# Second mixer: the strips alternate between two pairs of accumulator banks, and the state's projections and one more output turn go to the three rotating banks

## The chip, the cores and the metric

The kernel runs on one core of a Trainium2 chip, as one launch. Its time is the device time of that launch in microseconds. The core has a matrix engine (TensorE, PE in the rows), a vector engine (VectorE, DVE), an activation engine (ScalarE, ACT), a general engine (GpSimd, POOL), and a queue that issues the transfers (SyncE, SP). TensorE writes only to PSUM, which has eight banks of 128 partitions x 512 float32 values; VectorE and ScalarE read the banks. The engines run each its own program in its own order, and wait for one another on semaphores.

## The reference, cut to what matters

The whole computes two blocks on 256 tokens of width 1024: a first block of two layers (feed-forward, a mixer, cross attention, feed-forward) and a second block. The change lies in the mixer of the second block:

```python
h = rms_norm_2(x, norm_mix[l])
qa, ka, va, u, qm, km, vm, gates = split_in(h @ w_in[l])
oa = swa_attention(qa, ka, va, sinks, slopes_swa)      # window of 128, 8 heads, a sink per head
ya = oa @ w_o_swa[l]
ys = s5_ssm(u, lam_re, lam_im, log_step, b_re, b_im, c_re, c_im, d_skip)   # 32 groups x 64 complex states
z = jax.nn.gelu(ys) @ w_glu[l]
yb = (z[..., :512] * jax.nn.sigmoid(z[..., 512:])) @ w_o_ssm[l]
om = moba_attention(qm, km, vm, slopes_moba)           # one block of 256 keys, 8 heads
yc = om @ w_o_moba[l]
g = jax.nn.sigmoid(gates)                              # three gates of width 1024
x = x + (g[..., :1024] * ya + g[..., 1024:2048] * yb + g[..., 2048:] * yc) @ w_out[l]
```

The reshapes to heads are left out. After it come a feed-forward layer with a squared ReLU and the last norm.

## The kernel before, in words

**Products.** Every weight is used in two halves, a high one (`whi`) and a low one (`wlo`), and a product of activations and weights is three matmuls (high by high, low by high, high by low: lines 445 to 447). Weights come in pieces of 128 x 1024 values: SyncE loads a piece into one of five buffers `raw`, ScalarE copies its high half (line 1118), VectorE subtracts to get the low half (line 1677), and TensorE multiplies. There are three buffers for the halves. Each engine's program makes the halves of piece j + 2 while TensorE is to work on piece j.

**Strips.** A strip is 512 columns of an output for all 256 tokens. A strip of kind `both` has two row blocks t = 0, 1 of 128 tokens, each of which accumulates in one bank over all of the strip's pieces, so it holds a pair of banks. `gemm_piece` (line 449) runs one piece; at a strip's first piece it takes the pair that it is told, or `next_pair()`.

**Who holds a bank.** `open_bank(b)` makes TensorE wait for the events in `free[b]`, the signals by which the last user's reader said that it is done, and `free[b]` is set when a user has issued its last matmul. `turn_bank()` hands out three rotating banks in turn. In the second mixer these are banks 3, 4 and 5; bank 7 holds the weighed values; before the change bank 6 is the state projections' own, and the strips go round the pairs (1, 2), (0, 1), (2, 0).

**The second mixer** (`second`, line 963 for TensorE, 1530 for ScalarE, 2472 for VectorE). After the strip `su` comes a loop over `MIXED`, 40 weight pieces s = 0 to 39 in a fixed order: sk (0, 1), sqa (2 to 5), sv (6, 7), sqm (8 to 11), the strips of the gates gate0 (12 to 15), gate1 (16 to 19), gate4 (20 to 23), gate5 (24 to 27), gate2 (28 to 31), gate3 (32 to 35), and swa0 (36, 37), swa1 (38, 39). Each of the four engines walks over the same s, and does beside the piece what the tables say:
- `DRIVEN_AT`: at every even s from 2 to 32 a drive k (0 to 15), the input matmuls of a state group (line 1030). VectorE reads its bank twice (lines 2533, 2534, event `back`), GpSimd combines, VectorE scans (2544), rotates (2547, 2548), GpSimd combines.
- `SCORED_AT`: at every even s from 8 to 30 the scores of an attention item (line 582). VectorE reads the bank (line 1856, event `biased`) and takes the maxima; ScalarE exponentiates (line 1207). At s + 1 TensorE transposes the probabilities (`prob_turn`, line 564), ScalarE copies them out at its s + 2 (line 1226, event `copied_a`), and at s + 3 TensorE weighs the values (line 611).
- Four drives later, after pieces 12, 20, 28 and 36, `project(J)` (line 1035, matmuls of line 1042) projects four state groups, and VectorE reads the result one step later (line 2552, event `scan`).
- `OUT_AT`: after pieces 24, 25, 35 and 36 TensorE transposes half an attention output (`out_turn`, line 544). ScalarE takes the high half out (line 1163), VectorE the low one (line 1768, event `alo`).
- After a gate strip's last piece ScalarE copies its two banks out, with the row scale or straight with the sigmoid (line 1552, event `gate`). Gelu and sigmoid need another activation table than the exponential.

Within an even s TensorE opens the drive's bank, then the score's, and only then issues the two kinds of matmuls by turns; the piece, `project`, the weighing, the transposes and the output turn follow in this order. After the loop come the strips glu1, glu0, moba0, ssm0, moba1, ssm1 and the output projection so0, so1, on the pairs (0, 1) and (2, 3), with rotating banks 4, 5 and 6.

Of the kernel before, what the change touches and what calls it, by code (L numbers as in the profile page):

```python
# [412 lines left out]
def pe_program(K, G, A):  # L413

    S, T = K.S, K.nc.tensor
    pe = Engine(T)
    ident, banks = K.ident, K.banks
    free = [()] * 8
    turn_n, pair_n, pairs = [0], [0], [((0, 2), (1, 3))]

    def open_bank(b):
        for event in free[b]:
            pe.wait_ge(*event)
        free[b] = ()

    def turn_bank():
        turn_n[0] += 1
        b = (3 if len(pairs[0]) == 3 else 4) + turn_n[0] % 3
        open_bank(b)
        return b  # L430

# [48 lines left out]
    def gemm(name, after0, after1, pair=None, beside={}):  # L480

        g = G[name]
        for n in range(g.n):
            gemm_piece(g, n, pair)
            if n in beside:
                beside[n]()
        free[K.place[name][0]], free[K.place[name][1]] = (after0,), (after1,)
# [473 lines left out]
        project_x("o", "oo", "x1")  # L961

    def second():
        pairs[0], pair_n[0] = ((1, 2), (0, 1), (2, 0)), 1
        gemm("su", S.copied_d.at(("su", 0)), S.copied_d.at(("su", 1)), None, {0: lambda: norm_turns("s", "f3", True, (2, 3))})
        b = turn_bank()
        K.place["spread"] = b
        for t in range(2):
# [37 lines left out]
        def mixed_piece(name, n):  # L1006
            if name in ("sk", "sv"):
                (keys_piece if name == "sk" else values_piece)(n)
                return
            gemm_piece(G[name], n, (2, 0) if name[:2] == "sq" else None)  # L1010
            if n == G[name].n - 1:
                for t in range(2):
                    free[K.place[name][t]] = ((S.gate.at((int(name[4]), t)) if name[:4] == "gate" else
                                               S.gated.at((0, int(name[3]), t)) if name[:3] == "swa" else S.copied_a.at((name, t))),)
# [18 lines left out]
                free[b] = (S.back.at(k),)  # L1033

        def project(J):
            open_bank(6)
            pe.wait_ge(*S.proj.at(0))
            pe.wait_ge(*S.turned_forth.at(4 * J + 3))
            for ri in range(2):
                for k in range(4 * J, 4 * J + 4):  # L1040
                    cs = slice(32 * BLOCKS[k % 4], 32 * BLOCKS[k % 4] + 32)
                    ins = T.matmul(banks[6][cs, 0:256], K.CL[ri][:, J, cs], K.state[k % 7][:, ri, :], start=ri == 0, stop=ri == 1,
                                   skip_group_check=True)
            ins.then_inc(*S.projected.done(J))
            free[6] = (S.scan.at(("z", J)),)
        for s, (name, n) in enumerate(MIXED):
            k = DRIVEN_AT.get(s)
            if k is not None and k != 1:
# [21 lines left out]
                prob_turn("mA" if i >= 6 else "sA", i % 6, 4)  # L1070
            if s in OUT_AT:
                a, _, g = OUT_AT[s]
                spare = [b for b in range(3) if b not in K.place[name]] if s == 25 else [None]
                out_turn(a, 0, K.O, lambda t, g: S.weighed.at((a, t)), (g,), spare[0])

        def gated(branch):
            return [[S.gated.at((branch, c, t)) for t in range(2)] for c in range(2)]
        pairs[0] = ((0, 1), (2, 3))
        gemm("glu1", S.silu.at(("glu", 0)), S.silu.at(("glu", 1)))
        gemm("glu0", S.product.at(("glu", 0)), S.product.at(("glu", 1)))  # L1080
        gemm("moba0", *gated(2)[0])
# [581 lines left out]
def dve_program(K, G, A):  # L1663
# [3 lines left out]
    banks = K.banks  # L1667
# [804 lines left out]
    def second():  # L2472
# [76 lines left out]

        def state_out(J):  # L2550
            dve.wait_ge(*S.projected.at(J))
            V.scalar_tensor_tensor(out=zin[:, J, :], in0=K.uT[:, J, :], scalar=K.gain(108 + J), in1=banks[6][:, 0:256],
                                   op0=ALU.mult, op1=ALU.add).then_inc(*S.scan.done(("z", J)))
        r8 = K.stat("r8", 2)
        for s, (name, n) in enumerate(MIXED):
# [402 lines left out]
```

## Time and profile before

| | us |
|---|---|
| median of three timed runs | 1626.81 |
| lowest, highest | 1624.32, 1627.30 |
| the profiled execution's own time | 1623.05 |
| its span | 1621.8 |
| TensorE busy | 1595.5 (98%) |
| VectorE busy | 1109.3 (68%) |
| ScalarE busy | 861.6 (53%) |
| GpSimd busy | 227.5 (14%) |

The span is that of one profiled execution, from its first to its last instruction; the time around it is 1.25 us more. Matmuls are pipelined: a matmul's own duration is longer than the distance to the next one's start, so the distances between starts tell how fast TensorE goes, and a short hole can stand there without showing as idle. A row's bracket gives the idle time of the engine before it and what ended it. In the timeline a row merges several like instructions (x2, x4).

### The profile page before, as it was taken

The page shows a single profiled execution, that of the slowest core. Times are in us where ns is not written, and L with a number is a line of the kernel's source. Part 1 is how long each engine was busy: PE and PEld are TensorE (multiplying, and loading weights), DVE is VectorE, ACT ScalarE, POOL GpSimd, SP SyncE. Part 2 cuts the span into 40 slices and gives each one's busy share as a digit, 9 for nine tenths or more (in the row PEclk, how much of TensorE's full clock was granted, in tenths as well). Part 3 has the DMA queues.
Part 4 walks back from the last instruction along what each step waited for, and adds up shares of the span by engine and source line. Part 5 has one row for each costly group of instructions (what it writes and reads, how often), then busy time and mean ns, then how long its engine had stood idle before and what let it go on. Part 6 is the DMA issues. An engine that isn't in the chain of part 4 may idle for free.

```text
span 1621.8 us, 21203 instructions
## 1 busy us (share of the span) xinstructions
PE 1595.5 (98%) x8050; PEld 1331.2 (82%) x8050; DVE 1109.3 (68%) x1769; ACT 861.6 (53%) x1324; POOL 227.5 (14%) x351
## 2 busy tenths in 40 slices
PE   8999999999999999999999999999999999999998
PEld 6888877788888888888889888888889877888886
DVE  6775788867655556555596775655568997776566
ACT  5554556855545445444555555544454457454444
POOL 2499901000000000000000000000014442100000
PEclk9999999999999999999999999999999999999999
DMA  9766656445455565655654553555685554556563
GB/s 283 242 208 213 207 169 191 150 142 156 140 185 188 188 186 178 191 185 190 213 171 156 163 186 111 183 187 187 189 261 166 165 157 143 182 194 193 188 188 109
DMA packets 187543, 295.22 MB, mean 182 GB/s; under 512 B 13510, under 2 KB 108144, under 8 KB 186160
## 3 DMA queue, kind: packets, MB, share of 16 engines
q1 hardware_dynamic: 183264, 275.93, 54.4%
q0 software_dynamic: 3888, 17.60, 3.4%
q8 instruction: 64, 1.05, 0.3%
q10 hardware_dynamic: 288, 0.33, 0.1%
q14 instruction: 39, 0.32, 0.1%
HBM read 288.29 MB, written 5.25 MB: 181 GB/s over the span
## 4 chain that ended last, share of the span: by engine, by line
PE 86%; DVE 8%; ACT 3%; issue 2%; POOL 1%; DMA 0%; SPq 0%; DVEq 0%; ACTq 0%
PE b L445 25%; PE b L447 24%; PE b L446 24%; PE b L667 4%; DVE wlo L1677 2%; PE b L669 2%; ACT whi L1118 1%; PE b L690 1%; PE b L920 1%; PE b L902 1%; PE b L511 1%; PE b L527 1%; PE b L611 1%; PE b L564 1%; ACT R L1207 1%
## 5 line engine op out<-in xcount | busy, mean ns | idle before, releaser
L1677 DVE TENSOR_TENSOR wlo<-raw,whi 128x1024 fp32r<-128x1024 f32 (+1 forms) x523 | 648.7, 1243 | 430.6 <-ACT whi L1118 429.2
L1118 ACT ACTIVATE whi<-raw 128x1024 fp32r<-128x1024 f32 (+1 forms) x523 | 549.8, 1053 | 554.3 <-PE b L447 518.4
L445 PE MATMUL b<-whi,hT 128*128 128x512 f32 (+1 forms) x1040 | 413.0, 397 | 9.4 <-DVE wlo L1677 8.2
L447 PE MATMUL b<-whi,hT 128*128 128x512 f32 (+1 forms) x1040 | 404.8, 389 | 0.0
L446 PE MATMUL b<-wlo,hT 128*128 128x512 f32 (+1 forms) x1040 | 404.3, 389 | 0.0
L445 PE MATMUL b<-whi,oT 128*128 128x512 f32 x672 | 265.1, 394 | 0.0
L447 PE MATMUL b<-whi,oT 128*128 128x512 f32 x672 | 262.0, 390 | 0.0
L446 PE MATMUL b<-wlo,oT 128*128 128x512 f32 x672 | 261.6, 389 | 0.0
L445 PEld LDWEIGHTS b<-whi,hT 128*128 128x128 f32 x1040 | 195.8, 188 | 54.7 <-DVE wlo L1677 10.4
L447 PEld LDWEIGHTS b<-whi,hT 128*128 128x128 f32 x1040 | 195.7, 188 | 41.6
L446 PEld LDWEIGHTS b<-wlo,hT 128*128 128x128 f32 x1040 | 196.0, 188 | 37.7
L447 PEld LDWEIGHTS b<-whi,oT 128*128 128x128 f32 x672 | 126.1, 188 | 26.9
L445 PEld LDWEIGHTS b<-whi,oT 128*128 128x128 f32 x672 | 126.2, 188 | 26.2 <-DVE R L2501 0.5
L446 PEld LDWEIGHTS b<-wlo,oT 128*128 128x128 f32 x672 | 126.3, 188 | 25.3
L667 PE MATMUL b<-hT,whi 128*128 128x512 f32 x256 | 90.8, 399 | 0.0
L1207 ACT ACTIVATE R<-R,st 128x256 f32<-128x256 f32 (+1 forms) x96 | 43.5, 455 | 73.3 <-DVE st L1861 30.5
L669 PE MATMUL b<-hT,wlo 128*128 128x256 f32 x256 | 71.9, 281 | 0.0
L2822 POOL DMA_DIRECT2D biasB<-in_rel x1 | 0.5, 527 | 490.8 <-PE b L690 490.8
L1249 ACT ACTIVATE biasA<-b,st 128x256 f32<-128x256 f32 x88 | 41.1, 474 | 44.6 <-PE b L447 41.2
L445 PE MATMUL b<-hT,whi 128*128 128x256 f32 (+1 forms) x216 | 62.2, 288 | 0.1
L446 PE MATMUL b<-hT,whi 128*128 128x256 f32 (+1 forms) x216 | 61.1, 283 | 0.0
L447 PE MATMUL b<-hT,wlo 128*128 128x256 f32 (+1 forms) x216 | 61.0, 283 | 0.0
(349 smaller groups left out, 1855.9 us busy)
## 6 DMA issues: line engine op xcount, KB each, us to landing
raw<-in_ffn_w_in SPq DMA_DIRECT2D x350, 256.0 KB, 3.2
raw<-in_ffn_w_out SPq DMA_DIRECT2D x88, 512.0 KB, 3.4
raw<-in_w_ff SPq DMA_DIRECT2D x64, 512.0 KB, 4.0
raw<-in_w_in SPq DMA_DIRECT2D x36, 512.0 KB, 3.7
raw<-in_x_w_kv SPq DMA_DIRECT2D x32, 512.0 KB, 4.1
raw<-in_even_w_in SPq DMA_DIRECT2D x24, 512.0 KB, 4.2
raw<-in_odd_w_in SPq DMA_DIRECT2D x24, 512.0 KB, 4.0
raw<-in_x_w_q SPq DMA_DIRECT2D x16, 512.0 KB, 4.1
```

Source lines behind the costliest of these rows:

```text
L445: T.matmul(out, ah, bh, start=start, stop=False, skip_group_check=skip)
L446: T.matmul(out, ah, bl, start=False, stop=False, skip_group_check=skip)
L447: return T.matmul(out, al, bh, start=False, stop=stop, skip_group_check=skip)
L511: ins = T.transpose(banks[b][:, (2 * i + t) * P:(2 * i + t + 1) * P], src[:, t, kt * P:(kt + 1) * P], ident)
L527: ins = T.transpose(banks[b][:, i * P:(i + 1) * P], K.sqj[t][:, i * P:(i + 1) * P], ident)
L564: ins = T.transpose(banks[b][:, k * P:(k + 1) * P], src[:, k * P:(k + 1) * P], ident)
L667: T.matmul(bank[:, :].rearrange("p (a t) -> p a t", a=2), hi[:, kk, cs], K.hs[:, :, kt, :], start=kt == 0, stop=False, skip_group_check=True)
L669: ins = T.matmul(bank[:, 256:512], lo[:, kk, cs], K.hT[0][:, kt, :], start=False, stop=kt == 7, skip_group_check=True)
L1118: E.activation(K.whi[j % NSPLIT][:, 0:n], K.raw[j % NRAW][:, 0:n], ACT.Copy).then_inc(*S.whi.done(j))
L1207: ins = E.activation(s3[:, h, :], s3[:, h, :], ACT.Exp, bias=nm[:, h:h + 1], accum_out=sm[h])
L1249: E.activation(s[:, 0:256], bank[:, 0:256], ACT.Silu, scale=K.stat(("y", f.name), 2)[:, t:t + 1]).then_inc(*S.silu.done((f.name, c, t)))
L1677: V.tensor_tensor(K.wlo[j % NSPLIT][:, 0:n], K.raw[j % NRAW][:, 0:n], K.whi[j % NSPLIT][:, 0:n].bitcast(F32), ALU.subtract).then_inc(*S.wl ...
```

## The change

The pairs of the second mixer's strips become (0, 1) and (2, 6), used by turns. `su` is told the pair (2, 0), which it had before, sqa is told (6, 0) instead of (2, 0), and sqm (2, 6). The keys and values stay in bank 1. `project(J)` takes `turn_bank()` instead of bank 6, and VectorE's `state_out` reads it from there. The output turn after piece 25, which took the one of banks 0 to 2 that no strip held, takes `turn_bank()` too. The first rotating bank is kept in `turn_first` and not worked out from the number of pairs. Since `su` no longer takes a pair from the rotation and there are two pairs and not three, the strips after the loop start on the other of their two pairs. No engine's instructions change or move; what changes is the bank in them and the waits ahead of them.

```diff
--- before.py
+++ after.py
@@ -416,7 +416,7 @@
     pe = Engine(T)
     ident, banks = K.ident, K.banks
     free = [()] * 8
-    turn_n, pair_n, pairs = [0], [0], [((0, 2), (1, 3))]
+    turn_n, turn_first, pair_n, pairs = [0], [4], [0], [((0, 2), (1, 3))]
 
     def open_bank(b):
         for event in free[b]:
@@ -425,7 +425,7 @@
 
     def turn_bank():
         turn_n[0] += 1
-        b = (3 if len(pairs[0]) == 3 else 4) + turn_n[0] % 3
+        b = turn_first[0] + turn_n[0] % 3
         open_bank(b)
         return b
 
@@ -961,8 +961,8 @@
         project_x("o", "oo", "x1")
 
     def second():
-        pairs[0], pair_n[0] = ((1, 2), (0, 1), (2, 0)), 1
-        gemm("su", S.copied_d.at(("su", 0)), S.copied_d.at(("su", 1)), None, {0: lambda: norm_turns("s", "f3", True, (2, 3))})
+        pairs[0], pair_n[0], turn_first[0] = ((0, 1), (2, 6)), 1, 3
+        gemm("su", S.copied_d.at(("su", 0)), S.copied_d.at(("su", 1)), (2, 0), {0: lambda: norm_turns("s", "f3", True, (2, 3))})
         b = turn_bank()
         K.place["spread"] = b
         for t in range(2):
@@ -1007,7 +1007,7 @@
             if name in ("sk", "sv"):
                 (keys_piece if name == "sk" else values_piece)(n)
                 return
-            gemm_piece(G[name], n, (2, 0) if name[:2] == "sq" else None)
+            gemm_piece(G[name], n, {"sqa": (6, 0), "sqm": (2, 6)}.get(name))
             if n == G[name].n - 1:
                 for t in range(2):
                     free[K.place[name][t]] = ((S.gate.at((int(name[4]), t)) if name[:4] == "gate" else
@@ -1033,16 +1033,16 @@
                 free[b] = (S.back.at(k),)
 
         def project(J):
-            open_bank(6)
+            b = K.place["project", J] = turn_bank()
             pe.wait_ge(*S.proj.at(0))
             pe.wait_ge(*S.turned_forth.at(4 * J + 3))
             for ri in range(2):
                 for k in range(4 * J, 4 * J + 4):
                     cs = slice(32 * BLOCKS[k % 4], 32 * BLOCKS[k % 4] + 32)
-                    ins = T.matmul(banks[6][cs, 0:256], K.CL[ri][:, J, cs], K.state[k % 7][:, ri, :], start=ri == 0, stop=ri == 1,
+                    ins = T.matmul(banks[b][cs, 0:256], K.CL[ri][:, J, cs], K.state[k % 7][:, ri, :], start=ri == 0, stop=ri == 1,
                                    skip_group_check=True)
             ins.then_inc(*S.projected.done(J))
-            free[6] = (S.scan.at(("z", J)),)
+            free[b] = (S.scan.at(("z", J)),)
         for s, (name, n) in enumerate(MIXED):
             k = DRIVEN_AT.get(s)
             if k is not None and k != 1:
@@ -1070,12 +1070,11 @@
                 prob_turn("mA" if i >= 6 else "sA", i % 6, 4)
             if s in OUT_AT:
                 a, _, g = OUT_AT[s]
-                spare = [b for b in range(3) if b not in K.place[name]] if s == 25 else [None]
-                out_turn(a, 0, K.O, lambda t, g: S.weighed.at((a, t)), (g,), spare[0])
+                out_turn(a, 0, K.O, lambda t, g: S.weighed.at((a, t)), (g,))
 
         def gated(branch):
             return [[S.gated.at((branch, c, t)) for t in range(2)] for c in range(2)]
-        pairs[0] = ((0, 1), (2, 3))
+        pairs[0], turn_first[0] = ((0, 1), (2, 3)), 4
         gemm("glu1", S.silu.at(("glu", 0)), S.silu.at(("glu", 1)))
         gemm("glu0", S.product.at(("glu", 0)), S.product.at(("glu", 1)))
         gemm("moba0", *gated(2)[0])
@@ -2549,7 +2548,7 @@
 
         def state_out(J):
             dve.wait_ge(*S.projected.at(J))
-            V.scalar_tensor_tensor(out=zin[:, J, :], in0=K.uT[:, J, :], scalar=K.gain(108 + J), in1=banks[6][:, 0:256],
+            V.scalar_tensor_tensor(out=zin[:, J, :], in0=K.uT[:, J, :], scalar=K.gain(108 + J), in1=banks[K.place["project", J]][:, 0:256],
                                    op0=ALU.mult, op1=ALU.add).then_inc(*S.scan.done(("z", J)))
         r8 = K.stat("r8", 2)
         for s, (name, n) in enumerate(MIXED):
```

TensorE's order at the transposes of piece 25 and the drive and score of piece 26, before (L611 weighs, L564 transposes the probabilities, L544 is the output turn, L1030 the drive, L582 the score; b0 to b7 are the banks):

```order
L611 MATMUL b7<-R1 128x64 x4
L564 MATMUL b5<-cst,R1 128x128 [waits s_exped,s_back]
L564 MATMUL b5<-cst,R1 128x128 x3
L544 MATMUL b0<-cst,O 128x128 [waits s_gate]
L544 MATMUL b0<-cst,O 128x128 x3
L1030 MATMUL b3<-vsb,BT 128x256 [waits s_alo,s_biased]
L582 MATMUL b4<-R1 128x256
L1030 MATMUL b3<-vsb,BT 128x256
L582 MATMUL b4<-R1 128x256
```

and after:

```order
L611 MATMUL b7<-R1 128x64 x4
L564 MATMUL b4<-cst,R1 128x128 [waits s_exped,s_back]
L564 MATMUL b4<-cst,R1 128x128 x3
L544 MATMUL b5<-cst,O 128x128 [waits s_biased]
L544 MATMUL b5<-cst,O 128x128 x3
L1030 MATMUL b3<-vsb,BT 128x256 [waits s_copied_a,s_alo]
L582 MATMUL b4<-R1 128x256
L1030 MATMUL b3<-vsb,BT 128x256
L582 MATMUL b4<-R1 128x256
```

The output turn (L544) has moved from bank 0 to bank 5. The probabilities are in bank 4 instead of 5, and that is the bank that the score of piece 26 takes next, so the drive's wait has gained `s_copied_a`.

TensorE's order between the projection after piece 12 and the drive and score of piece 14 (the twelve matmuls of piece 13 and L1042, the projection, stand before this), before:

```order
L611 MATMUL b7<-R1 128x64 [waits s_copied_a]
L611 MATMUL b7<-R1 128x64 x3
L564 MATMUL b4<-cst,R1 128x128 [waits s_exped]
L564 MATMUL b4<-cst,R1 128x128 x3
L1030 MATMUL b5<-vsb,BT 128x256 [waits s_biased,s_back]
L582 MATMUL b3<-R1 128x256
L1030 MATMUL b5<-vsb,BT 128x256
L582 MATMUL b3<-R1 128x256
```

and after, where L1042 is in bank 4 instead of 6:

```order
L611 MATMUL b7<-R1 128x64 x4
L564 MATMUL b5<-cst,R1 128x128 [waits s_exped,s_back]
L564 MATMUL b5<-cst,R1 128x128 x3
L1030 MATMUL b3<-vsb,BT 128x256 [waits s_scan,s_biased]
L582 MATMUL b4<-R1 128x256
L1030 MATMUL b3<-vsb,BT 128x256
L582 MATMUL b4<-R1 128x256
```

The drive went from bank 5 to 3 and the score from bank 3 to 4, the projection's bank, and the wait has gained `s_scan`. The same stands at pieces 22 and 30.

TensorE's order at the first piece of gate3 (piece 32), before:

```order
L1030 MATMUL b3<-vsb,BT 128x256 [waits s_back]
L1030 MATMUL b3<-vsb,BT 128x256
L445 MATMUL b2<-whi2,hT 128x512 [waits s_gate,s_wlo]
L446 MATMUL b2<-wlo2,hT 128x512
L447 MATMUL b2<-whi2,hT 128x512
L445 MATMUL b0<-whi2,hT 128x512 [waits s_gate]
L446 MATMUL b0<-wlo2,hT 128x512
```

and after:

```order
L1030 MATMUL b4<-vsb,BT 128x256 [waits s_back]
L1030 MATMUL b4<-vsb,BT 128x256
L445 MATMUL b2<-whi2,hT 128x512 [waits s_gate,s_wlo]
L446 MATMUL b2<-wlo2,hT 128x512
L447 MATMUL b2<-whi2,hT 128x512
L445 MATMUL b6<-whi2,hT 128x512 [waits s_gate]
L446 MATMUL b6<-wlo2,hT 128x512
```

The second row block went from bank 0, which gate2 had just filled, to bank 6, which gate5 had. Both waits are for `s_gate`, but for different values of it.

## Rows read from the trace of the kernel before

**Rows 1.** The page's part 1: busy us, share of the span, instructions

```profile
PE 1595.5 (98%) x8050; PEld 1331.2 (82%) x8050; DVE 1109.3 (68%) x1769; ACT 861.6 (53%) x1324; POOL 227.5 (14%) x351
```

**Rows 2.** Busy time by stretch: length, each engine's busy us, TensorE's clock, DMA

```profile
1205.00:1377.00 172.00, 168.42 (x1092) 142.12 (x1091) 154.65 (x243) 96.71 (x186) 64.98 (x80) 1.00 0.55 165
```

**Rows 3.** Waits of TensorE, 1205 to 1440: total us, times, longest

```profile
PE b L445 <- ACT biasB L1552: 1.2, 1, 1.2
```

**Rows 4.** Timeline, pieces 25 and 26: start, duration, engine, line [idle before <-releaser]

```profile
1323.29 0.60 PE L544 MATMUL b<-cst,O 128*128 128x128 f32 x4
1323.59 0.68 DVE L1768 TENSOR_TENSOR oT<-b,oT 128x512 fp32r<-128x512 f32 x1
1323.93 0.60 ACT L1163 ACTIVATE oT<-b 128x512 fp32r<-128x512 f32 x1 [1.42 <-PE b L544]
...
1324.42 0.45 PE L1030 MATMUL b<-vsb,BT 64*128 64x256 f32 x1 [0.53 <-DVE oT L1768]
1324.42 1.05 ACT L1118 ACTIVATE whi<-raw 128x1024 fp32r<-128x1024 f32 x1
...
1325.37 0.58 ACT L1226 ACTIVATE R<-b 128x512 f32<-128x512 f32 x1
```

**Rows 5.** Timeline, drive of piece 14 and the first projection's read

```profile
1273.27 0.48 PE L1030 MATMUL b<-vsb,BT 64*128 64x256 f32 x1
...
1273.30 0.48 DVE L2552 SCALAR_TENSOR_TENSOR vsb<-vsb,gcol,b 128x256 f32<-128x256 f32 x1
...
1274.02 0.38 PE L1030 MATMUL b<-vsb,BT 64*128 64x256 f32 x1
...
1274.84 0.69 DVE L2533 TENSOR_TENSOR R<-b,M 128x512 f32<-128x512 f32 x1
```

**Rows 6.** Timeline, drive of piece 22 and the second projection's read

```profile
1306.51 0.48 DVE L2552 SCALAR_TENSOR_TENSOR vsb<-vsb,gcol,b 128x256 f32<-128x256 f32 x1
...
1306.72 0.48 PE L1030 MATMUL b<-vsb,BT 64*128 64x256 f32 x1
```

**Rows 7.** Timeline, drive of piece 30 and the third projection's read

```profile
1340.41 0.48 DVE L2552 SCALAR_TENSOR_TENSOR vsb<-vsb,gcol,b 128x256 f32<-128x256 f32 x1
...
1341.77 0.48 PE L1030 MATMUL b<-vsb,BT 64*128 64x256 f32 x1
```

**Rows 8.** Timeline, first products of gate3 (piece 32) and gate2's copies

```profile
1351.43 0.40 PE L447 MATMUL b<-whi,hT 128*128 128x512 f32 x1
...
1352.31 1.27 ACT L1552 ACTIVATE biasB<-b,st 128x512 f32<-128x512 f32 x2
...
1353.05 0.50 PE L445 MATMUL b<-whi,hT 128*128 128x512 f32 x1 [1.23 <-ACT biasB L1552]
...
1353.39 0.39 PE L446 MATMUL b<-wlo,hT 128*128 128x512 f32 x1
...
1353.62 0.40 PE L447 MATMUL b<-whi,hT 128*128 128x512 f32 x1
```

**Rows 9.** Timeline, low half of piece 35 and TensorE's first product of it

```profile
1359.52 1.22 DVE L1677 TENSOR_TENSOR wlo<-raw,whi 128x1024 fp32r<-128x1024 f32 x1
...
1361.62 0.39 PE L445 MATMUL b<-whi,hT 128*128 128x512 f32 x1
```

**Rows 10.** Timeline, first products of swa1 (piece 38)

```profile
1372.36 0.39 PE L447 MATMUL b<-whi,oT 128*128 128x512 f32 x1
...
1372.80 0.50 PE L445 MATMUL b<-whi,oT 128*128 128x512 f32 x1
```

**Rows 11.** Timeline, two products near the start, and a wait of TensorE at 208 us

```profile
7.15 0.63 PE L445 MATMUL b<-whi,hT 128*128 128x512 f32 x1
7.58 0.63 PE L446 MATMUL b<-wlo,hT 128*128 128x512 f32 x1
...
208.29 1.38 PE L511 MATMUL b<-cst,O 128*128 128x128 f32 x8 [2.22 <-DVE O L1747]
```

**Rows 12.** Busy time of the stretch 205 to 210 us, columns as in rows 2

```profile
205.00:210.00 5.00, 2.72 (x16) 1.94 (x15) 4.48 (x17) 2.52 (x3) 0.87 (x2) 1.00 0.52 213
```

## The prediction

> **What bounds the kernel now.** I read the page first. TensorE is busy 98% of the span [rows 1], so a change in the second mixer can move the end only through time in which TensorE stands still there. The busy time by stretches shows the mixer: between 1205 and 1377 us TensorE is busy for 168.42 of 172.00 us, VectorE for 154.65, at a granted clock of 1.00 [rows 2]. So TensorE leads, VectorE follows with 90%, and at most 3.6 us are there to be won, of which the waits name the owners: 1.2 us for a gate copy of ScalarE (a strip's bank) [rows 3], 0.5 us for a low half of VectorE (a rotating bank) [rows 4]; one more wait, for a softmax exponential, hangs on data and not on a bank, and the change leaves it alone. Then I laid the waits which the change writes against the timeline: for every bank, when its old user lets go of it, and when TensorE comes to it.
>
> The weight pieces of the mixer have the numbers 0 to 39 here, in their order in MIXED. TensorE issues twelve 128x512 products for a piece, 0.23 us apart (1353.39, 1353.62) [rows 8].
>
> **Strips on two pairs (removes waits).** Before, neighbouring strips share one of the banks 0, 1, 2, so a strip's second row block must wait for the copy out of the strip before. That costs time at one place, the start of gate3 (piece 32): the product at 1351.43 would be followed by one at 1351.66, but it comes at 1353.05, when the first of the two gate activations that start at 1352.31 is over [rows 8]. 1353.05 - 1351.66 = 1.39 us. After, gate3 has banks 2 and 6, whose last user was gate5, a whole strip earlier. ScalarE does not get faster by it, though: the weight chain for the pieces behind was set by ScalarE and GpSimd. The low half of piece 35's weights is written by VectorE from 1359.52 to 1360.74, and TensorE takes piece 35 at 1361.62 [rows 9]. If TensorE is 1.39 us ahead it comes at 1360.23 and must wait until about 1360.74 + 0.15 = 1360.89: 0.66 us are given back. (0.15 us is what lay between the end of VectorE's low half, 1323.59 + 0.68 = 1324.27, and TensorE's start at 1324.42 [rows 4].) What stands before that low half on VectorE works on the state and waits for GpSimd and ScalarE there, not for TensorE, so it does not move up with it. Net gain 0.73 us; bounds 0 (all given back) and 1.39 (nothing).
> A smaller one of the same kind is at swa1 (piece 38): 1372.80 after 1372.36 instead of 1372.59 [rows 10], 0.21 us, because bank 1 was still swa0's. After, swa1 has gate3's banks, which ScalarE has emptied during swa0. Gain 0.21 us; bounds 0 and 0.21. The other strip starts show no idle time before, and lose only waits that were met.
>
> **The state's projections in a rotating bank (adds waits).** Project had bank 6 for itself. Now it takes the next of 3, 4, 5, and a rotating bank comes round after three takers. Project(J) is issued after pieces 12, 20 and 28, and the third taker after it is the score of pieces 14, 22 and 30. In program order that score's wait stands before the drive matmul (both banks are opened first), so TensorE stands still with the drive too until VectorE has read the projection (L2552).
> First: VectorE ends it at 1273.30 + 0.48 = 1273.78, TensorE starts the drive at 1273.27 [rows 5]. New start 1273.78 + 0.15 = 1273.93, cost 0.66 us.
> Second: 1306.51 + 0.48 = 1306.99 against 1306.72 [rows 6], alone 0.42 us with the 0.15. But TensorE is then already 0.66 us late and VectorE less so: its next read of a drive bank (1274.84) has to wait for the drive that ended at 1274.02 + 0.38 = 1274.40, now 0.66 later, plus an estimated 0.1 us for the release, 1275.16, so VectorE slips by 0.32 [rows 5]. 0.42 + 0.32 - 0.66 = 0.08 us.
> Third: 1340.41 + 0.48 = 1340.89 against 1341.77 [rows 7]: met, 0.9 us to spare.
> Together 0.74 us; bounds 0 (if the release comes well before the end that the profile shows) and 1.08 (0.66 + 0.42, if VectorE slips as far as TensorE). The two other new waits of this part are met by far: project itself wants a copy of ScalarE that is long done, and the transposes of the probabilities want VectorE's read of a drive bank, which stands a whole piece earlier in its order.
>
> **The output turn of piece 25 in a rotating bank (adds the largest wait).** Before, it took a free strip bank (bank 0 in the order's rows). Now it is one more taker between the probabilities' transposes of the same piece and the drive and score of piece 26. So the score of piece 26 gets the bank whose probabilities TensorE has only just transposed, and ScalarE must have copied them out. ScalarE is busy in that order: it takes the high half of the output turn (1323.93, it waited for TensorE's transposes from 1323.29), then the high half of a weight piece (1324.42), and copies the probabilities from 1325.37 to 1325.95 [rows 4]. TensorE starts piece 26's drive at 1324.42, having already waited 0.5 us for the low half of the other output turn. ScalarE's release reaches TensorE fast (two gate activations from 1352.31 take 0.7 us for the first, and TensorE goes on at 1353.05 [rows 8]), so 0.04 us are added: 1325.95 + 0.04 - 1324.42 = 1.57 us. ScalarE's three instructions all hang on TensorE's own transposes, so the wait moves along with whatever TensorE lost before; nothing else in the way hides it. Bounds: 0.62 (if the weight piece between, 1324.42 to 1325.37, fell out of the chain) and 1.98 (with as much again as a piece's first product comes late by after such a wait, 1353.39 - 1353.05 - 0.23 = 0.11 us [rows 8], and the 0.3 us by which VectorE slipped at piece 14). While TensorE stands, VectorE runs dry too: its read of the drive's result waits for the later drive. VectorE is then closer behind TensorE, which is why the third projection stays met; it does not cost on its own, since the weights' low halves are made two pieces ahead.
>
> **Sum.** 0.74 + 1.57 - 0.73 - 0.21 = +1.37 us. On the profiled execution's own 1623.05 us (span 1621.8) that gives 1624.4. The three timed runs have a median of 1626.81, 3.8 us above that execution, and I add the difference to it: 1626.81 + 1.37 = 1628.2 us, +0.08%. From no change this kernel's measurement can tell about 0.2%, 3.3 us (the three runs alone differ by 3 us), so the forecast is: no change that shows, on the slow side of it.
>
> The Trainium skill, "Perfetto Trace Analysis", section "Matmuls", says that independent matmul groups should rotate through different PSUM banks, so that the emptying of one overlaps the next one's products. By that rule the change would gain the whole 1.39 us of gate3 and cost nothing. The trace agrees with it for the strips, but the same rule speaks against the other half of the change, which puts five more groups on the same three banks.
>
> **Rivals.**
> A, the gain stays whole and the new waits are short. For it: only one bank wait of the mixer has a price above 1 us now [rows 3], and ScalarE has idle time in the mixer, so it may come to the copy earlier. Against it: three instructions of ScalarE in a row, of which the first waits for TensorE [rows 4]. It gives -1.39 - 0.21 + 0.62 = -0.98 us, 1625.8 us.
> B, VectorE becomes the bound. With 154.65 of 172.00 us busy [rows 2] it has little room, and each of TensorE's new waits starves it (0.3 us at piece 14, more at piece 26). If as much as the wait at piece 26 costs, 1.57 us, comes back once more as waits of TensorE for low halves of weights, and piece 35 eats up all of gate3's gain, the sum is 0.74 + 1.57 - 0.21 + 1.57 = +3.7 us: 1630.5, slower. It decides from the point where a low half ends less than 0.1 us before TensorE wants it; at 1360.74 against 1361.62 [rows 9] there are 0.88 us, elsewhere more, and that speaks against it.
> C, the clock falls. At piece 26 TensorE would be idle from 1323.29 + 0.60 = 1323.89 to 1325.99, 2.1 us. At the lower level the products come every 0.43 us (7.15, 7.58) instead of 0.23 [rows 11]; if the 24 products of pieces 26 and 27 ran so, that is 24 x 0.20 = 4.8 us more, +6.2 in all, 1633.0 us. Against it: before 208.29 TensorE waited 2.22 us and the granted clock of that stretch is 1.00 [rows 11, 12]. The Trainium skill, "TensorE: Matmul & The Clock Gate", section "HAM oscillation — how this bites in real kernels", says that idle gaps between bursts of matmuls can throttle the clock; this trace shows none that did so by its length.
>
> **How the numbers follow.** Forecast 0.74, A 0.14, B 0.08, C 0.04. The likeliest time is 1628.2. The terms' bounds give 0 + 0.62 - 1.39 - 0.21 = -0.98 to 1.08 + 1.98 - 0 - 0 = +3.1, and a median of a few runs moves by 1 us or so by itself: 1625.2 to 1631.0, which takes in A and B and leaves out C. Faster by over 0.2% would need 3.3 us, more than all bank waits of the mixer hold: 0.03, for the scatter alone. Slower by over 0.2%: C, half of B, and some scatter on top of a forecast that is already at +1.4: 0.13. Within: 0.84.
>
> **What would show it.** In the profile after: TensorE's drive of piece 26 waits for ScalarE's copy of the probabilities (L1226) for about 2 us where it waited 0.5 us for VectorE; the drives of pieces 14 and 22 wait for VectorE's projection read, about 0.6 and 0 us; the wait for the gate activation at gate3 is gone and a wait for the low half of weights of about 0.6 us has come two or three pieces later; the granted clock stays at 1.00. If no wait for L1226 shows at piece 26, the largest term is wrong; if low halves are waited for at more than one place, it is B.

## The result, and the profile after

| us | before | after |
|---|---|---|
| median (executions) | 1624.79 (12) | 1626.83 (12) |
| lowest, highest | 1622.57, 1627.30 | 1625.63, 1629.15 |
| the profiled execution's own time | 1623.05 | 1626.74 |
| its span | 1621.8 | 1625.4 |
| its mean granted clock | 0.999 | 0.997 |

The ratio is 1.0016, with a 95% interval of [1.0009, 1.0024]: 0.0016 x 1625 = 2.6 us slower, a loss clear of the scatter but within the 0.2% that the forecast called no change. A second comparison, with the same kernel on another occasion, gave 1.0020 [1.0012, 1.0029] (e0_again below). The forecast was +1.37 us and 1628.2 us. The time itself came out 1.4 us below the forecast although the loss came out larger, and that the two are so close is luck: the three runs on which the forecast stood (median 1626.81) were long ones for this kernel, whose medians in the comparisons are 1624.79, 1623.59 and 1623.40. The base was 1626.81 - 1624.79 = 2.0 us too high, while the loss by medians, 2.04 us, was 0.7 us more than forecast. One of the 33 executions of the kernel before that stand beside e3, e4, e5 and e7 took 1987.04 us at a granted clock of 0.753, and the ratios leave it out.

Lines of VectorE and ScalarE have a number lower by one in the kernel after: L1225 copies the probabilities, L2551 reads the projection, L1676 writes the low halves. The page's part 1, after, against [rows 1]:

```profile
PE 1598.0 (98%) x8050; PEld 1334.1 (82%) x8050; DVE 1109.2 (68%) x1769; ACT 861.7 (53%) x1324; POOL 227.5 (14%) x351
```

The instructions are the same, and yet TensorE is busy 2.5 us longer: waits alone would have made it stand still, not work longer. Some matmuls must have run slower. The busy time by stretches, with the granted clock as the third number from the end, shows where; the row of 1205 to 1377 us answers to [rows 2], and before has 1.00 in every one of these stretches:

```profile
206.00:212.00 6.00, 3.73 (x13) 3.01 (x13) 5.57 (x15) 4.43 (x7) 0.26 (x1) 0.73 0.67 226
328.00:334.00 6.00, 5.17 (x29) 4.28 (x29) 5.85 (x11) 3.10 (x7) 0.00 (x0) 1.00 0.31 90
...
1205.00:1377.00 172.00, 166.64 (x1081) 140.70 (x1079) 152.21 (x240) 94.66 (x185) 64.93 (x80) 0.99 0.56 164
...
1328.00:1330.00 2.00, 2.00 (x11) 1.20 (x8) 0.96 (x2) 0.00 (x0) 0.05 (x1) 0.58 0.95 314
1330.00:1332.00 2.00, 2.00 (x7) 1.57 (x6) 1.93 (x5) 0.00 (x0) 1.43 (x2) 0.56 0.21 81
1332.00:1334.00 2.00, 2.00 (x11) 1.64 (x10) 2.00 (x3) 1.42 (x5) 0.00 (x0) 1.00 0.00 0
```

The clock has fallen at two places, near 208 us and at piece 26. TensorE's waits inside the mixer, after, against [rows 3]:

```profile
PE b L1030 <- ACT R L1225: 2.2, 1, 2.2
PE b L564 <- ACT st L1215: 1.6, 1, 1.6
PE b L1030 <- DVE vsb L2551: 0.8, 2, 0.6
PE b L445 <- DVE wlo L1676: 0.5, 1, 0.5
```

The gate's wait (1.2 us, biasB) is gone. The wait for the softmax exponential (L1215) is the one that hangs on data, and has stayed at 1.6. The other three rows are the new ones of the prediction. Their places in the timeline, against [rows 5], [rows 6], [rows 7], [rows 4], [rows 8], [rows 9] and [rows 10] in that order (rows between those shown are left out, here and below):

```profile
1273.93 0.47 DVE L2551 SCALAR_TENSOR_TENSOR vsb<-vsb,gcol,b 128x256 f32<-128x256 f32 x1
1274.55 0.45 PE L1030 MATMUL b<-vsb,BT 64*128 64x256 f32 x1 [0.57 <-DVE vsb L2551]
...
1307.69 0.47 DVE L2551 SCALAR_TENSOR_TENSOR vsb<-vsb,gcol,b 128x256 f32<-128x256 f32 x1
1308.31 0.45 PE L1030 MATMUL b<-vsb,BT 64*128 64x256 f32 x1 [0.27 <-DVE vsb L2551]
...
1344.66 0.48 DVE L2551 SCALAR_TENSOR_TENSOR vsb<-vsb,gcol,b 128x256 f32<-128x256 f32 x1
1346.48 0.48 PE L1030 MATMUL b<-vsb,BT 64*128 64x256 f32 x1
...
1324.80 0.60 PE L544 MATMUL b<-cst,O 128*128 128x128 f32 x4
1324.97 0.68 DVE L1767 TENSOR_TENSOR oT<-b,oT 128x512 fp32r<-128x512 f32 x1
1325.44 0.60 ACT L1162 ACTIVATE oT<-b 128x512 fp32r<-128x512 f32 x1 [1.56 <-PE b L544]
1325.93 1.05 ACT L1117 ACTIVATE whi<-raw 128x1024 fp32r<-128x1024 f32 x1
1326.88 0.59 ACT L1225 ACTIVATE R<-b 128x512 f32<-128x512 f32 x1
1327.61 0.45 PE L1030 MATMUL b<-vsb,BT 64*128 64x256 f32 x1 [2.21 <-ACT R L1225]
1328.95 0.79 PE L445 MATMUL b<-whi,hT 128*128 128x512 f32 x1
1329.54 0.63 PE L446 MATMUL b<-wlo,hT 128*128 128x512 f32 x1
...
1356.14 0.40 PE L447 MATMUL b<-whi,hT 128*128 128x512 f32 x1
1356.38 0.40 PE L445 MATMUL b<-whi,hT 128*128 128x512 f32 x1
...
1364.22 1.22 DVE L1676 TENSOR_TENSOR wlo<-raw,whi 128x1024 fp32r<-128x1024 f32 x1
1365.49 0.50 PE L445 MATMUL b<-whi,hT 128*128 128x512 f32 x1 [0.50 <-DVE wlo L1676]
...
1376.39 0.39 PE L447 MATMUL b<-whi,oT 128*128 128x512 f32 x1
1376.61 0.39 PE L445 MATMUL b<-whi,oT 128*128 128x512 f32 x1
```

The first product of gate3's second row block comes 0.24 us after the one before it (1356.14, 1356.38), where there were 1.62 us, and at swa1 the product that came 0.44 us after its neighbour comes 0.22 us after it (1376.39, 1376.61): both strips find their banks empty. Such a comparison is read by distances: one takes the start of the same matmul in both traces, and where the difference changes, time was lost or won. That gives this account of 3.69 us between the two profiled executions (1626.74 - 1623.05):

| place | start before, after | difference | changes by | predicted |
|---|---|---|---|---|
| on entering the mixer (clock, 208 us) | | 0.64 | +0.64 | not the change's |
| drive of piece 14 | 1273.27, 1274.55 | 1.28 | +0.64 | +0.66 |
| drive of piece 22, and what it gave back | 1306.72, 1308.31 | 1.59, then 1.51 | +0.23 | +0.08 |
| output turn, drive of piece 26 | 1324.42, 1327.61 | 3.19 | +1.68 | +1.57 |
| drive of piece 30 (clock, piece 26) | 1341.77, 1346.48 | 4.71 | +1.52 | 0 |
| gate3, with piece 34 as the place it is read | | 3.21 | -1.50 | -1.39 |
| past piece 35's first product | | 4.02 | +0.81 | +0.66 |
| past swa1, to the end | | 3.68 | -0.34 | -0.21 |

Without the two rows of the clock it is 0.64 + 0.23 + 1.68 - 1.50 + 0.81 - 0.34 = +1.52 us, where +1.37 was forecast.

### The profile page after: what moved, and what is told of

The parts are those of the page before. It is cut to its first block and busy times, and to the rows that moved or that the text cites. A ratio compares the mean times of both kernels' runs of the same rounds, so it can differ in the third digit from the quotient of the medians.

```text
span 1625.4 us, 21204 instructions
## 1 busy us (share of the span) xinstructions
PE 1598.0 (98%) x8050; PEld 1334.1 (82%) x8050; DVE 1109.2 (68%) x1769; ACT 861.7 (53%) x1324; POOL 227.5 (14%) x351
## 5 line engine op out<-in xcount | busy, mean ns | idle before, releaser
L1676 DVE TENSOR_TENSOR wlo<-raw,whi 128x1024 fp32r<-128x1024 f32 (+1 forms) x523 | 648.6, 1243 | 430.7 <-ACT whi L1117 429.6
```

The lines of the kernel that those rows point to most:

```text
L1676: V.tensor_tensor(K.wlo[j % NSPLIT][:, 0:n], K.raw[j % NRAW][:, 0:n], K.whi[j % NSPLIT][:, 0:n].bitcast(F32), ALU.subtract).then_inc(*S.wl ...
```

## The experiments

Theory: the time after is the sum of the three kinds of waits as forecast, and on top of it the granted clock falls behind the long wait at piece 26 and costs some 1.5 us. Rival: the wait alone costs what is seen, and the lower clock is another of the falls that this kernel has anyhow, at one place or another, whatever the change does. Each kernel was timed in five rounds against the kernel before. Since falls of the clock come and go between executions, I look in each profile at the clock at three places: 206 to 212 us, 328 to 334 us, and about piece 26.

**e0_again**: the changed kernel once more, unedited.

> The changed kernel once more, beside the others, for its time on this chip and for a second profile. Theory (wait and clock): it takes 2 to 3.5 us more than before; TensorE waits 2.2 us for the copy of line 1225 at piece 26, and the granted clock falls to about 0.57 for 3 to 4 us behind it, so that some six products come 0.43 us apart. Rival (the fall was an accident of one execution): the wait is there, the clock stays at 1.00, and the time is 1.5 us less than in the profile, +1.4 us over before.

Median 1627.5 (11 executions, lowest 1625.63), before 1623.59 (31, lowest 1622.72), ratio 1.0020 [1.0012, 1.0029]. The clock is 1.00 at the first two places, and falls again at piece 26:

```profile
206.00:212.00 6.00, 3.71 (x21) 3.05 (x20) 5.58 (x15) 4.50 (x7) 0.11 (x1) 1.00 0.68 240
...
1326.00:1328.00 2.00, 1.06 (x6) 0.98 (x8) 0.73 (x2) 0.79 (x2) 1.40 (x2) 0.72 0.93 229
1328.00:1330.00 2.00, 2.00 (x9) 1.16 (x6) 0.93 (x2) 0.00 (x0) 0.00 (x0) 0.50 0.76 285
1330.00:1332.00 2.00, 2.00 (x10) 1.63 (x9) 1.93 (x5) 0.00 (x0) 1.44 (x2) 0.92 0.00 0
```

This execution took 1626.11 us. It enters the mixer without the 0.64 us of the first one, so its distance from before is the change's own: 3.06 us, which is 1.52 for the waits and 1.5 for the clock. Here the low stretch begins with the drive of piece 26 and ends some 3.5 us later.

**e1_turn25_strip**: the output turn of piece 25 back in a strip bank, the rest as after.

```diff
-                out_turn(a, 0, K.O, lambda t, g: S.weighed.at((a, t)), (g,))
+                out_turn(a, 0, K.O, lambda t, g: S.weighed.at((a, t)), (g,), 0 if s == 25 else None)
```

> The changed kernel with the output turn of piece 25 in bank 0 (of the pair that no strip holds then). Theory: the wait for line 1225 goes (1.7 us) and with it the fall of the clock (1.5 us): 3.2 us less than the changed kernel, about 0.3 us less than before. Rival 1 (the copy of the probabilities is not what sets piece 26, the low half of the other output turn ends last anyway): less than 1 us gained. Rival 2 (the clock falls for another reason, such as the many small transposes there): 1.7 us gained, and the slow products stay in the profile.

Median 1623.46 (lowest 1622.40), ratio 1.0002 [0.9993, 1.0011]. The wait for L1225 is gone, and so is the fall of the clock. Its waits in the mixer, but for the softmax's:

```profile
PE b L1030 <- DVE vsb L2551: 0.8, 2, 0.6
PE b L445 <- DVE wlo L1676: 0.5, 1, 0.5
PE b L1030 <- DVE oT L1767: 0.4, 1, 0.4
```

and its stretch at piece 26:

```profile
1328.00:1330.00 2.00, 2.00 (x11) 1.62 (x10) 1.97 (x4) 0.00 (x0) 1.42 (x3) 1.00 0.93 313
```

Against e0_again that is 4.0 us by medians, 3.2 by the fastest runs and 0.0018 x 1624 = 2.9 by ratios. The wait accounts for 1.68 of it. So this one bank choice carries the loss of the change; the rest of it comes out even as far as the interval tells, and by distances in the profile it wins 0.3 us (0.62 us behind the kernel before just ahead of the drive of piece 14, 0.32 after the mixer).

**e2_turn25_only**: the kernel before, with nothing but this output turn in a rotating bank.

```diff
-                spare = [b for b in range(3) if b not in K.place[name]] if s == 25 else [None]
-                out_turn(a, 0, K.O, lambda t, g: S.weighed.at((a, t)), (g,), spare[0])
+                out_turn(a, 0, K.O, lambda t, g: S.weighed.at((a, t)), (g,))
```

> The kernel before with one part of the change alone: the output turn of piece 25 takes a rotating bank. Theory: that part alone costs the wait of 1.6 us and, if TensorE stands still as long as in the changed kernel, the fall of the clock of 1.5 us: +3.1 us over before, so more than the whole change. Rival (by the prediction's own sum): +1.57 us, clock at 1.00.

Median 1627.83 (9 executions, lowest 1626.02), ratio 1.0017 [1.0007, 1.0028]. The wait is there without the rest of the change. The profile names VectorE's low half as its releaser, but that name is wrong. The rotation lets the drive and score of piece 26 wait for two things: the low half of piece 24's output turn, which was done at 1327.03 + 0.68 = 1327.71, and ScalarE's copy of the probabilities, done at 1328.81 + 0.59 = 1329.40. The low half that ends at 1328.76 + 0.68 = 1329.44 is that of piece 25's turn, in a bank for which nothing waits here; it only happens to end last:

```profile
1326.74 0.60 PE L544 MATMUL b<-cst,O 128*128 128x128 f32 x4
1327.03 0.68 DVE L1767 TENSOR_TENSOR oT<-b,oT 128x512 fp32r<-128x512 f32 x1
...
1328.76 0.68 DVE L1767 TENSOR_TENSOR oT<-b,oT 128x512 fp32r<-128x512 f32 x1
1328.81 0.59 ACT L1225 ACTIVATE R<-b 128x512 f32<-128x512 f32 x1
1329.55 0.45 PE L1030 MATMUL b<-vsb,BT 64*128 64x256 f32 x1 [2.21 <-DVE oT L1767]
```

and here the clock did not fall behind the same 2.21 us, although it had fallen at both of the earlier places:

```profile
206.00:212.00 6.00, 3.72 (x14) 2.81 (x14) 5.55 (x16) 4.14 (x7) 0.54 (x1) 0.75 0.62 209
328.00:334.00 6.00, 5.62 (x13) 4.01 (x14) 5.82 (x11) 3.10 (x7) 0.00 (x0) 0.54 0.29 96
...
1330.00:1332.00 2.00, 2.00 (x13) 1.45 (x11) 1.26 (x3) 0.00 (x0) 0.11 (x1) 1.00 0.94 313
```

The account closes all the same. The output turn is 1326.74 - 1323.29 = 3.45 us behind [rows 4], almost all of it from the early falls; the drive of piece 26 comes 1329.55 - 1324.42 = 5.13 behind, so the wait costs 1.68, and 1623.05 + 5.13 = 1628.2 is the time of this execution (1628.27). The ratio's 0.0017 x 1624 = 2.8 us is near the 3.1 expected, but its interval also takes in the rival's 1.57, and in this profile the rival is right about piece 26: the wait cost 1.68 us and the clock stayed. What made this execution long beyond that were the falls at the two other places, which the edit does not touch.

**e6_filled_wait**: the changed kernel, with TensorE kept at work during the wait: two float32 products of the identity with constants into the drive's own bank, which the drive then overwrites (the profile lists them as x4, at line 1052).

```diff
                 drive_open(k)
+                if s == 26:
+                    for _ in range(2):
+                        T.matmul(banks[K.place["drive", k]][:, :], ident, K.cst[:, 0:512], start=True, stop=True)
```

> The changed kernel with two extra float32 products (128x128 by 128x512, of constants, into the drive's bank, overwritten by the drive) between the output turn of piece 25 and the drive of piece 26: TensorE works through most of its wait, some 1.7 us at 0.85 us a product (a guess from four passes of 0.21 us), and the release of the score's bank comes at the same time as before. Theory (the fall of the clock follows from the idle time): the granted clock stays at 1.00, the drive starts within 0.2 us of where it did, and the time is 1.5 us less than the changed kernel although it does more work. Rival (the clock falls for another reason, or the wait itself is the whole price): the same time as the changed kernel or more.

```profile
1327.45 0.60 PE L544 MATMUL b<-cst,O 128*128 128x128 f32 x4
1328.37 1.99 PE L1052 MATMUL b<-cst 128*128 128x512 f32 x4 [0.31 <-DVE oT L1770]
1330.28 0.48 PE L1030 MATMUL b<-vsb,BT 64*128 64x256 f32 x1
```

The drive starts 2.83 us after the output turn, where it was 2.81 without the filling (1324.80, 1327.61): the wait has its full length still, only it isn't idle. And the clock stays:

```profile
1328.00:1330.00 2.00, 1.69 (x5) 0.68 (x4) 2.00 (x3) 1.91 (x3) 1.98 (x4) 1.00 0.35 109
1330.00:1332.00 2.00, 2.00 (x12) 1.26 (x12) 0.54 (x2) 0.12 (x1) 0.72 (x2) 1.00 0.74 207
```

Median 1626.37 (lowest 1624.47), ratio 1.0011 [1.0002, 1.0020]. That is 0.0009 x 1624 = 1.5 us less than e0_again by ratios, 1.1 by medians and 1.2 by the fastest runs. The two intervals overlap, and one profile with the clock at 1.00 is no proof either, since e2's had it behind the same wait unfilled. The single executions say more. Five of e6's eleven (1624.47 to 1625.30) are below 1625.63, the shortest of 23 executions of the unfilled kernel. And the record gives the mean granted clock of every execution: it is 0.999 in the profiles without a fall (before, e4, e5), 0.998 in those with one of some 3.5 us (e0, e1), and lower with more. All 32 executions with the unfilled wait (after, e0, e2) have 0.998 or less; two of e6's eleven have 0.999, and so have 22 of the 63 of before that stand beside these runs. So products that do nothing useful win back at least part of what the fall cost, and leave the wait's 1.68.

**e3_project_only**: the kernel before, with the projections in rotating banks.

```diff
         def project(J):
-            open_bank(6)
+            b = K.place["project", J] = turn_bank()
...
-            free[6] = (S.scan.at(("z", J)),)
+            free[b] = (S.scan.at(("z", J)),)
```

The matmuls of the projection and VectorE's read take the same bank b; their lines are not shown.

> The kernel before with one part of the change alone: the state's projections take a rotating bank. Theory: TensorE's drives of pieces 14 and 22 wait for VectorE's read of the projection, +0.65 and +0.3 us as in the changed kernel, the third is met; in all +0.7 to +1.0 us over before. Rival (VectorE, kept waiting, falls behind and low halves come late): a new wait for a low half of weights, over +1.5 us.

Median 1624.36 (lowest 1623.55), before 1623.40 (33 executions, lowest 1622.36), ratio 1.0004 [0.9995, 1.0014]. Waits in the mixer, again without the softmax's, and without 0.4 us for the output turn of piece 24:

```profile
PE b L445 <- ACT biasB L1552: 1.2, 1, 1.2
PE b L1030 <- DVE vsb L2552: 0.8, 2, 0.6
```

The two waits of the projections are here, gate3's is still there, and none for a low half has come. +0.96 by medians, which the interval can't tell from nothing. The waits can, and so can the distances: 1.89 us behind the kernel before just ahead of the drive of piece 14, 2.61 after the mixer, +0.7. The rival's new low half is not there.

**e4_strips_only**: only the strips' new pairs. From e1, with the projections back in bank 6 (which the strips now use too, so each waits for the other's reader).

```diff
-            b = K.place["project", J] = turn_bank()
+            b = K.place["project", J] = 6
+            open_bank(b)
```

> The strips on two pairs alone: the changed kernel with project in bank 6 (of the pair that no strip holds then) and the output turn of piece 25 in bank 0. Theory: gate3's wait for the gate activation goes (-1.5 us), the wait for the low half of piece 35 comes (+0.8), the wait at swa1 goes (-0.3): about -1.0 us against before and 0.9 less than the kernel that has only the output turn put back. Rival A of the prediction (the gain stays whole): -1.7 us and no wait for a low half.

Its waits, without the softmax's and the 0.5 us for the output turn of piece 24 that before has too:

```profile
PE b L445 <- DVE wlo L1677: 0.5, 1, 0.5
```

Median 1622.36 (lowest 1621.64), ratio 0.9995 [0.9986, 1.0005]: -1.0 by medians, which the interval can't tell from nothing either. By distances in the profile it is 0.26 us behind the kernel before at the drive of piece 14 and 0.83 us in front of it after the mixer: -1.09. The wait for the low half comes with the strips' pairs and with nothing else, as the prediction has it: e3 has gate3's wait and no low half's, e4 the reverse.

**e5_strips_both_turns**: e4, with the output turn of piece 24 also in a strip bank that is free at that point.

```diff
-                out_turn(a, 0, K.O, lambda t, g: S.weighed.at((a, t)), (g,), 0 if s == 25 else None)
+                out_turn(a, 0, K.O, lambda t, g: S.weighed.at((a, t)), (g,), {24: 0, 25: 1}.get(s))
```

> The strips alone as in the kernel beside it, and both output turns of pieces 24 and 25 in the pair that no strip holds (banks 0 and 1), so that the drive of piece 26 no longer waits for the low half of line 1767. Theory: another 0.5 us less, about -1.5 us against before, and a stretch without any wait for a bank. Rival (what is won at piece 26 is given back as a longer wait for the low half of piece 35 or for an exponential): no gain over the strips alone.

Median 1622.02 (lowest 1621.12), ratio 0.9987 [0.9977, 0.9996]. The wait of 0.5 us for VectorE's copy of the output turn, which the kernel before has at piece 26, is gone as well: in its profile the drive starts 0.53 us behind that output turn (1323.62, 1324.15), where it was 1.13.

```profile
1323.62 0.60 PE L544 MATMUL b<-cst,O 128*128 128x128 f32 x4
1324.15 0.48 PE L1030 MATMUL b<-vsb,BT 64*128 64x256 f32 x1
```

It beats both kernels: by 1.4 us the one before, and by some 5 the changed one (medians 1622.02 and 1627.5, of different comparisons). By distances it goes from 0.33 us behind the kernel before to 1.35 in front of it, -1.68, which is 0.6 more than e4. The intended idea, strips on two pairs, is worth 1 us by e4's medians and distances; it needed none of the two moves to rotating banks that came with it.

**e7_filled_206**: e5, with two throw-away products in the wait near 208 us as in e6.

```diff
+    def fill(b, n):
+        for _ in range(n):
+            T.matmul(banks[b][:, :], ident, K.cst[:, 0:512], start=True, stop=True)
...
             open_bank(b)
+            if (name, g) == ("e", 0):
+                fill(b, 2)
```

> The same as the strips with both output turns, and two extra float32 products of constants in front of the transposes at 208 us, in the bank that these overwrite, where TensorE stands still for 2.2 us in every kernel so far, and the clock fell in four of six profiles. Theory (idle time lets the clock fall in some executions, and that is much of the scatter of all these kernels): the clock stays at 1.00 between 206 and 218 us, the median is 0.4 us or so less than without the products, and the slower half of its runs comes down. Rival (the extra products delay the transposes, or heat and not idle time lets the clock fall): the same or more time, and the fall still there.

Median 1621.47 (lowest 1620.76), ratio 0.9992 [0.9983, 1.0001]. By the median it is 0.55 us faster than e5, by the ratio not at all, and its profiled execution took 1626.09:

```profile
206.00:212.00 6.00, 5.44 (x24) 3.53 (x23) 5.47 (x17) 2.89 (x3) 1.50 (x2) 1.00 0.54 218
328.00:334.00 6.00, 5.17 (x18) 3.61 (x17) 5.85 (x10) 3.10 (x7) 0.00 (x0) 0.64 0.28 87
```

The filled place kept its clock, but so it did unfilled in four of nine profiles. The unfilled place at 328 us did not keep it. This execution had a fall near its start as well (0.56 and 0.59 from 12 to 16 us, where the kernel before has 1.00), and came to 205 us 1.6 us late. As a test of the clock and as an improvement this run is inconclusive.

## Why the prediction was right, and what it missed

- *The projections* (0.74 forecast, 0.64 + 0.23 = 0.87 measured). The first is exact to 0.02 us. At the second VectorE had slipped further than the 0.32 us that I gave it: its read moved from 1306.51 [rows 6] to 1307.69, 1.18 us, of which 0.64 were there on entering, so 0.54. With it the same sum is 0.42 + 0.54 - 0.64 = 0.32, which TensorE shows (1.59 - 1.28 = 0.31), and 0.08 of it were made up by the end of piece 23. The third was met, with 1346.48 - 1344.66 - 0.48 = 1.3 us to spare. e3 shows both waits alone.
- *The output turn* (1.57 forecast, 1.68 measured). The chain is the one that was worked out: turn, ScalarE's high half of it 0.64 us later as before, a weight's high half, the probabilities. All four moved by the 1.51 us that TensorE was late, so nothing hid the wait. The missing 0.1 us is the release: 1327.61 - (1326.88 + 0.59) = 0.14, where I had read 0.04 from the gate activations. The drive's own bank was free at 1324.97 + 0.68 = 1325.65; it stood for the score's. e1 and e2 show that the term belongs to this edit alone, taken out and put in.
- *gate3 and what is given back* (-1.39 + 0.66, measured -1.50 + 0.81). The low half did not move up with TensorE: 1359.52 [rows 9] became 1364.22, 4.70 later, while TensorE had come from 4.71 down to 3.21. Both terms are 0.11 to 0.15 us larger because the product after a wait and the one behind it are 0.34 apart instead of 0.23 (1365.49, 1365.83), which I had counted only among the bounds.
- *swa1* (-0.21, measured -0.34), the same 0.1 us again.
- *The step that failed* is "the granted clock stays at 1.00". Rival C named the mechanism, with its place and cause, and gave it 0.04. I set against it one wait of 2.22 us, at 208 us, behind which the clock had stayed at 1.00 [rows 11, 12]. That execution proved only that such a wait need not lower the clock. The same place, unedited, in nine profiles of this study (all but e7): 1.00 in before, e0, e4 and e5, and 0.72 to 0.79 in after, e1, e2, e3 and e6. One profiled execution of a thing that comes and goes was taken for a rule. The fall at piece 26 stands in two of the three profiles with the unfilled wait and in none of the seven without it, and cost 1.5 us. What the forecast would have needed was a chance of a half or more, with 1.5 us behind it.
- C's size was three times too large for this place. 24 products at the lower level were supposed; in the profile after, the drive's last matmuls and some six products of piece 26 were slow (distances of 0.42 to 0.59 instead of 0.23 from 1328.95 on), and from 1332 us the clock is back at 1.00 with the same engine running the same products. Near 328 us falls of about that length and of twice that length were seen, the longer ones for 3.2 us.
- A fell as expected: e4, which has gate3's gain and none of the new waits, shows the low half's wait, so the gain is not whole even there. B did not come: the one low half is waited for, once, for 0.5 us.

The Trainium skill, "TensorE: Matmul & The Clock Gate", section "HAM oscillation — how this bites in real kernels", says that gaps between bursts of matmuls can throttle the clock. The prediction read this trace as speaking against that; the runs speak for it, with 0.58 and 0.50 behind the wait at piece 26 in two of three profiles, and 1.00 there in all seven profiles without such an idle wait.

What stays open: how often the clock falls at piece 26. Two of three profiles show it. The changed kernel's fastest execution of 23 is 1625.63, 3.3 us above before's 1622.36, and that is nearer to the sum with the fall (3.0) than without (1.5), so most executions seem to have it. The mean clocks agree, 0.998 or less in all 32 executions with the unfilled wait; but both are inferred, since only three were profiled, and a mean does not say where the clock fell. And what decides in a given execution whether a wait of this length lowers the clock was not found.

## What to carry to other kernels

Before work is moved to a rotating resource, write down in program order who takes each unit and whose read frees it: three units are enough for three takers between a write and its read, and the taker that comes one too early makes everything behind it in the engine's order stand, here a drive whose own bank had been free for 2 us. If a change combines a gain with moves that only make room for it, time the parts apart: here the gain (1 us) needed none of the moves, and one of these cost some 3 us, wait and clock together. And price a new wait of the matrix engine twice, for its length and for the clock behind it, and read the clock behind such a wait in several executions, not in one.

## What the runs showed of the hardware

- Whether the clock falls behind a given wait changes from one execution to the next. Near 208 us (wait of 2.2 us) it fell in five of nine profiles; near 328 us, behind two waits of 0.98 and 0.83 us in e7, it fell in four of ten (0.54 to 0.72); at piece 26 in two of three.
- Much of the scatter of this kernel is that. In the 63 executions of before, those with a mean granted clock of 0.999 took 1622.36 to 1624.42 us, those with 0.997 took 1624.72 to 1625.86, and those with 0.995 took 1628.05 to 1629.04.
- What a fall costs differs by the place. At piece 26 it was 1.5 us. Near 208 us it was 0.6 us in after and e1; in e2, e3 and e6 TensorE came to 326 us 0.29, 0.34 and 0.09 us behind the kernel before, no later than e4 and e5 without a fall (0.33 both), because a later wait took the delay up: TensorE's 0.64 us for VectorE near 278 us in before was gone in e2 and 0.2 in e3 and e6, while in after and e1 it stayed at 0.7. Near 328 us it was 3.2 us in e2 (0.29 us behind at 326 us, 3.47 at 337) and 1.6 in e3, where the clock was low for half as long.
- So short waits can be followed by a dearer fall than a long one: the price lies in the matmuls behind it, up to where the clock is back. At piece 26 products came 0.43 us apart until 1332 us, and the clock was low for some 3.5 us (0.58 and 0.56 from 1328 to 1332 us); near 328 us in e2 they came so from 330.34 to 335.20, behind two waits that are not 2 us together.
- With throw-away products in the wait, the clock stood at 1.00 in the one profile taken at each of the two places (piece 26 in e6, 206 to 212 us in e7), and the wait was not lengthened (2.83 against 2.81 us, e6). That they help at piece 26 is borne out by e6's executions; at 208 us it is not shown.
- TensorE went on 0.14 us after the end of ScalarE's copy at piece 26 (0.15 in e2: 1329.40, 1329.55), and 0.05 us after the end of VectorE's low half at piece 35 (1364.22 + 1.22 = 1365.44, 1365.49); the prediction had read 0.04 and 0.15 for the two engines. The end of an instruction in the profile gives the release to within 0.1 us only. And where two copies end within 0.05 us of each other, as in e2, the profile can name the wrong one; which of them the bank waits for is read from the kernel.
